# Moving four weight loads, a gather and a small table around the hand-over from the front part to the experts

## What is computed

```python
x = x + mix @ p['w_out']                       # output product, K = 1024
x = x + _moe(_rmsnorm(x, p['norm2_g']), p)

# _moe, for the tokens t (520 x 1024)
gl = t @ p['w_router_group'] + p['b_router_group']      # 4 groups, the best one
el = t @ p['w_router_expert'] + p['b_router_expert']    # 8 experts in it, the best two
...
for e in range(N_EXPERTS):                              # 32
    a = t @ p['w_gate'][e]                              # 1024 x 512
    u = t @ p['w_up'][e]                                # 1024 x 512
    out = out + combine[:, e:e + 1] * ((jax.nn.silu(a) * u) @ p['w_down'][e])
```

## Time and profile before

| | us |
|---|---|
| median of 3 executions | 777.6 (777.34 to 778.83) |
| the profiled execution's own time | 776.52 |
| its span, first to last instruction | 774.8 |
| PE busy | 668.8 (86%) |
| DVE busy | 272.4 (35%) |
| ACT busy | 160.7 (21%) |
| share of the span on the chain that ended last: PE, DMA, DVE | 46%, 34%, 9% |
| the weights' DMA queue (q1): moved, share of 16 engines | 233.95 MB, 75.3% |

### The profile page before, as it was taken

One profiled execution on the slowest core, in us unless ns is written; L12 is line 12 of the kernel. 1 busy time (PEld: TensorE's weight loads), 2 busy tenths in 40 slices (PEclk: granted clock), 3 DMA queues, 4 the chain that ended last, 5 costly groups with the idle time before them and its releaser, 6 DMA issues.

```text
span 774.8 us, 9756 instructions
## 1 busy us (share of the span) xinstructions
PE 668.8 (86%) x3294; PEld 333.8 (43%) x3294; DVE 272.4 (35%) x558; ACT 160.7 (21%) x314; POOL 89.4 (12%) x161
## 2 busy tenths in 40 slices
PE   6999989999996899999799987776778768888895
PEld 3488878954556533333233332222223322233231
DVE  7798994284476312121112121111111111112047
ACT  3677410421513001111001010010010101001023
POOL 4100000000000111212021211111121111021000
PEclk9999999999997799999999999999989999899998
DMA  9422016379217899999999999999999999999982
GB/s 332 183 109 110 1 53 278 117 290 383 91 61 287 309 353 377 412 389 415 382 419 397 408 412 408 415 406 411 413 393 415 401 412 408 402 403 415 422 331 110
DMA packets 29575, 246.56 MB, mean 318 GB/s; under 512 B 6578, under 2 KB 7090, under 8 KB 16592
## 3 DMA queue, kind: packets, MB, share of 16 engines
q1 hardware_dynamic: 22784, 233.95, 75.3%
q0 software_dynamic: 5280, 8.20, 3.1%
q10 hardware_dynamic: 1456, 3.62, 1.2%
HBM read 235.65 MB, written 19.20 MB: 329 GB/s over the span
## 4 chain that ended last, share of the span: by engine, by line
PE 46%; DMA 34%; DVE 9%; issue 3%; ACT 3%; PEldq 2%; ACTq 0%; PEld 0%; SPq 0%; POOLq 0%; DVEq 0%; POOL 0%
DMA mem<-in_w_down 33%; PE psA L1351 25%; PE psB L1351 20%; DVE mem L688 5%; PEldq L1684 2%; DMA mem<-hn_d,mem 1%; DVE mem L827 1%; PE psA L1356 1%; DVE mem L839 1%; ACT mem L629 1%; DVE mem L869 0%; DVE mem L870 0%; ACT front_c L618 0%; PEldq L1682 0%; ACT mem L566 0%
## 5 line engine op out<-in xcount | busy, mean ns | idle before, releaser
L1351 PE MATMUL psA<-mem 128*64 128x512 f32 (+8 forms) x1380 | 323.6, 528 | 43.6 <-DMA mem<-in_w_gu 12.4
L1351 PE MATMUL psB<-mem 128*64 128x512 f32 (+6 forms) x1242 | 274.4, 536 | 41.0 <-DMA mem<-in_w_gu 20.9
L1351 PEld LDWEIGHTS psA<-mem 128*64 128x64 f32 (+4 forms) x1380 | 154.2, 156 | 194.2 <-issue 163.8
L1351 PEld LDWEIGHTS psB<-mem 128*64 128x64 f32 (+2 forms) x1242 | 118.2, 153 | 178.9 <-issue 146.6
L688 DVE TENSOR_TENSOR mem<-mem 128x512 f32<-128x512 f32 (+18 forms) x121 | 66.0, 560 | 24.4 <-ACT mem L535 20.1
L1258 POOL DMA_INDIRECT y_d<-front_c,mem x30 | 27.5, 917 | 298.2 <-DVE front_c L1063 298.2
L1088 DVE TENSOR_TENSOR front_c<-front_c,psB 64x512 f32<-64x512 f32 x15 | 10.3, 690 | 136.1 <-ACT front_c L618 136.1
L1088 DVE TENSOR_TENSOR front_c<-front_c,psA 64x512 f32<-64x512 f32 x15 | 10.3, 690 | 124.6 <-ACT front_c L618 124.6
L1253 POOL DMA_INDIRECT mem<-hn_d,mem x34 | 33.4, 981 | 99.8 <-DMA hn_d<-mem 71.4
L618 ACT ACTIVATE front_c<-psA 64x512 f32<-64x512 f32 x15 | 8.8, 589 | 131.6 <-PE psA L1351 131.6
L618 ACT ACTIVATE front_c<-psB 64x512 f32<-64x512 f32 x15 | 8.8, 589 | 131.0 <-PE psB L1351 131.0
(11 more groups left out here) (232 smaller groups left out, 382.0 us busy)
## 6 DMA issues: line engine op xcount, KB each, us to landing
mem<-in_w_gu SPq DMA_DIRECT2D x64, 2048.0 KB, 36.6
mem<-in_w_down SPq DMA_DIRECT2D x32, 2048.0 KB, 41.8
mem<-in_w_out SPq DMA_DIRECT2D x2, 2048.0 KB, 8.4
y_d<-mem SPq DMA_DIRECT2D x1, 4096.0 KB, 11.8
mem<-y_d SPq DMA_DIRECT2D x8, 512.0 KB, 9.5
mem<-in_x_T SPq DMA_DIRECT2D x8, 260.0 KB, 8.7
mem<-in_w_vb SPq DMA_DIRECT2D x8, 256.0 KB, 8.9
mem<-in_x_prompt SPq DMA_DIRECT2D x4, 512.0 KB, 11.1
```

The lines of the kernel that those rows point to most:

```text
L1351: return nc.tensor.matmul(out, lhsT, rhs, start=start, stop=stop, skip_group_check=True)
```

## The change

Five things are moved.

1. SP issues `load(6)` after a new signal, `wo_used`: PE gives it when the last product that reads slot 6 is done, `out_half(3, 1, (1,))`. It no longer waits for the whole output product.
2. SP issues `load(7)` after the last store of `x2` and after the last logits (`lg_ps`), `load(8)` directly behind it once `hn2` is stored, and `load(9)` only when the rows of expert 0 have landed (`xg_in[0]`).
3. On PE the second table goes behind the turn of expert 0's rows. 12 matmuls of `keep_busy` stand ahead of the three register loads and 8 behind them; before, 8 stood ahead of the table and 14 behind the loads. The loads wait for the count alone (`xslot_rdy` 1), the table for both signals (`xslot_rdy` 2).
4. On DVE the copy of expert 0's turned rows goes ahead of `rows_of(tblx)`.
5. The signal `zero_rdy` is merged into `consts`; what waits for it waits for the same instruction as before.

The diff, without the list of semaphores that loses `zero_rdy`:

```diff
--- before.py
+++ after.py
@@ -242,6 +242,7 @@
         y_ps, y_ev, ya_rdy, sqa_rdy, suma_ps, rta_rdy, mixa_rdy = map(
             sem, "y_ps y_ev ya_rdy sqa_rdy suma_ps rta_rdy mixa_rdy".split())
         o_ps, o_ev, o_sc = sem("o_ps"), sem("o_ev"), sem("o_sc")
+        wo_used = sem("wo_used")
         n2sq, n2rt, hn2_rdy, rest_in, x2T_ps, x2T_ev, lg_ps, lg_ev, wr_rdy, rt_rdy = map(
             sem, "n2sq n2rt hn2_rdy rest_in x2T_ps x2T_ev lg_ps lg_ev wr_rdy rt_rdy".split())
         hn2_out = [sem(f"hn2_out{u}") for u in range(2)]
...
@@ -345,7 +346,7 @@
             for r in range(2):
                 sp.dma_start(o[2 + r], hfin[:, r]).then_inc(st_out, 16)
                 sp.dma_start(o[4 + r], hnew[:, r]).then_inc(st_out, 16)
-            sp.wait_ge(zero_rdy, 1)
+            sp.wait_ge(consts, 5)
             sp.dma_start(y2_d[0:1024, :].rearrange("(a p) n -> p a n", p=128), zeros.unsqueeze(1).to_broadcast([128, 8, D])).then_inc(zero_out, 16)
             sp.dma_start(y2_d[1024:2 * NTOK, :], zeros[0:2 * NTOK - 1024]).then_inc(zero_out, 16)
             sp.wait_ge(ub_ps, 4)
@@ -377,16 +378,17 @@
                 load(q)
             for n in range(NT - 1):
                 store_x2(n)
+            sp.wait_ge(wo_used, 1)
+            load(6)
+            store_x2(NT - 1)
             sp.wait_ge(o_ps, NT)
-            load(6)
+            sp.wait_ge(lg_ps, NT)
             load(7)
-            store_x2(NT - 1)
-
-            sp.wait_ge(lg_ps, NT)
             sp.wait_ge(hn2_out[0], 48)
             sp.wait_ge(hn2_out[1], 32)
             load(8)
             sp.wait_ge(x2_out, 16 * NT)
+            sp.wait_ge(xg_in[0], 16)
             load(9)
 
             for q in range(NSLOT, 3 * NE):
@@ -1037,7 +1039,7 @@
             link(V.tensor_scalar(xt, xt, MAGIC, None, ALU.add))
             link(V.tensor_scalar(xt, xt, -MAGIC, 0.0, ALU.add, ALU.max))
             link(V.tensor_tensor_scan(xs, one32, xt, 0.0, ALU.mult, ALU.add))
-            V.tensor_copy(xb[0:1, 1:NE + 1], xs[0:1])
+            V.tensor_copy(xb[0:1, 1:NE + 1], xs[0:1]).then_inc(xslot_rdy, 1)
             link(tt(d, xs, xt, ALU.subtract))
             link(tt(xprod, oh12.rearrange("p t j e -> p (t j) e"), d.unsqueeze(1).to_broadcast([128, 2 * NT, NE]), ALU.mult))
             first, tile = xtile[:, 0, :], xtile[:, 1, :]
@@ -1093,9 +1095,9 @@
                 x1 = dve.value_load(xb[0:1, bass.ds(s + 1, 1)], min_val=0, max_val=NX)
                 further(x0, x1, ps, other)
 
+            xT_copy(0, 0)
             dve.wait_ge(xtbl_ps, 1)
             rows_of(tblx, psA[:, 3, 128:512], NX + 1).then_inc(xtbl_rdy, 1)
-            xT_copy(0, 0)
             dve.wait_ge(xtbl_rdy, 1)
             dve.wait_ge(ex_out, 1)
             link(V.tensor_reduce(R(1), ex[:, :, 0:NG], AX.X, ALU.add))
@@ -1231,7 +1233,7 @@
             G.memset(H[:, :, :, NS:NS + 1], 0.0).then_inc(h0_rdy, 1)
 
             pool.wait_ge(s_ev, NH)
-            G.memset(zeros, 0.0).then_inc(zero_rdy, 1)
+            G.memset(zeros, 0.0).then_inc(consts, 1)
             pool.wait_ge(st_out, 16 * 5)
             pool.wait_ge(rta_rdy, 1)
             G.iota(tokens, [[1, NTOK]], base=0, channel_multiplier=0, allow_small_or_imprecise_dtypes=True).then_inc(tokens_rdy, 1)
@@ -1552,7 +1554,7 @@
             pe.wait_ge(lg_ev, 1)
             out_half(3, 1, (0,))
             turn(3, 2)
-            out_half(3, 1, (1,))
+            out_half(3, 1, (1,)).then_inc(wo_used, 1)
             logits(3, 2)
             out_half(3, 0, (0,))
             pe.wait_ge(slot_rdy, 2)
@@ -1581,7 +1583,7 @@
             pe.wait_ge(tbl_rdy, 1)
 
             def further_table():
-                pe.wait_ge(xslot_rdy, 1)
+                pe.wait_ge(xslot_rdy, 2)
                 for n, (t, j) in enumerate(itertools.product(range(NT), range(2))):
                     r = ROWS[t]
                     ins = mm(psA[0:C, 3, 128:128 + 2 * (NX + 1)], row_oh[0:r, t, j, :], xentry[0:r, 2 * t + j].rearrange("p x w -> p (x w)"),
@@ -1684,12 +1686,13 @@
                     pe.drain().then_inc(gu_used, 1)
                 further(x0, x1, ps, other, s, s + 2, half_used if split else None)
 
+            keep_busy(12)
+            pe.wait_ge(xslot_rdy, 1)
+            bounds = [pe.value_load(xb[0:1, k:k + 1], min_val=0, max_val=NX) for k in range(3)]
             keep_busy(8)
-            further_table()
-            bounds = [pe.value_load(xb[0:1, k:k + 1], min_val=0, max_val=NX) for k in range(3)]
-            keep_busy(14)
             pe.wait_ge(xg_in[0], 16)
             x_T(psA[:, 0, :], xg[0:C, 0, :]).then_inc(xgT_ps, 1)
+            further_table()
             tile_step(0, before=False, split=True)
             pe.wait_ge(cw3_rdy, 1)
             for n, (t, j) in enumerate(itertools.product(range(NT), range(2))):
```

More of the change, by code:

```diff
@@ L259, in build @@
         y_in = [sem(f"y_in{t}") for t in range(NT)]
-        x2_out, zero_rdy, zero_out, tokens_rdy, cw3_rdy, cw_ps, picks_rdy, rest_out, y_last = map(
-            sem, "x2_out zero_rdy zero_out tokens_rdy cw3_rdy cw_ps picks_rdy rest_out y_last".split())
+        x2_out, zero_out, tokens_rdy, cw3_rdy, cw_ps, picks_rdy, rest_out, y_last = map(
+            sem, "x2_out zero_out tokens_rdy cw3_rdy cw_ps picks_rdy rest_out y_last".split())
         f_acc, f_ps, f_sum, f_sq, f_rt, f_done, f_out = map(sem, "f_acc f_ps f_sum f_sq f_rt f_done f_out".split())
```

## The result

| | before | changed |
|---|---|---|
| median, 20 executions each (us) | 776.99 (775.01 to 781.43) | 771.11 (767.02 to 777.46) |
| ratio to before, 95% interval | | 0.9926 (0.9912 to 0.9941) |
| profiled execution / its span | 776.52 / 774.8 | 770.57 / 768.9 |

The change makes the kernel 5.9 us faster. The direction was right and the size was less than half of what came.

What follows compares the result with a forecast made beforehand. Bound by the weight stream, whose early loads follow expert 0's first transpose on PE: -2.6 there and +0.2 for the clock give -2.4 us, from a median of 777.6 to 775.2; range 772.8 to 777.7.

Steps and rivals of the forecast that it cites:

- What bounds the kernel: Weight stream, saturated from 290 to 730; ahead of it, whatever moves the first transpose moves the end by as much.
- PE up to the first transpose: From the fillers' start at 248.47 to expert 0's first transpose: at 257.8 and not 260.42, so -2.6 us.
- The register loads: Three on PE between the two groups of fillers: 1.43 us, as in the old chain, ending at 254.5.
- The 20 fillers: On PE ahead of the first transpose: first 8 take 2.95, four more 1.6, last 8 3.3 at the low clock.
- rival 1: PE's clock is up for the last fillers, transpose 3.7 to 4.9 us earlier: 773.3 us; chance 0.22.
- The gather: Expert 0's rows: starts at 249.4, lands between 252.8 and 258.3, taken as 254, hidden behind the fillers.
- Unit 6's place: Load issued at 223.37, 9.5 us ahead of 232.88, in a stretch of idle DMA: gain and cost 0.
- the hold on unit 9: Unit 9 held back until the gather lands; by the queue rule it buys the gather nothing.
- The clock behind the transposes: Transposes at the low clock cost 0 to 0.7 us more, taken as 0.2.
- rival 2: Clock comes back late, behind 257.8; gain shrinks to 1.6 or nothing: 776.9 us; chance 0.15.
- Rival 4: Earlier PE start is not passed on, stream short of something else up to 286: 777.6 us; chance 0.12.
- rival 3: Slower: low clock through expert 0's gate/up product, 14.8 and not 7.4, sum +5.5: 783 us; chance 0.06.

Runs made afterwards that it cites:

- e6: Changed kernel with 2 fillers ahead of the three register loads and 18 behind, not 12 and 8: 776.9 us, ratio 0.9997.
- e2: Changed kernel with the loads of units 6 to 9 where they stood before, only PE's and DVE's new order kept: 778.0 us, ratio 1.0022.
- e3: Changed kernel without unit 9's wait for the gather: 777.6 us, ratio 1.0014.
- e12: Changed kernel with 2 and not 8 fillers behind the register loads: 771.8 us, ratio 0.9923.
- e8: Changed kernel with units 8 and 9 both held for the gather, and 2 and not 8 fillers behind the register loads: 772.5 us, ratio 0.9931.
- e11: Changed kernel with unit 6 loaded only at the end of the output product, as before: 777.2 us, ratio 0.9997.
- e1: Kernel before with only SP's part of the change (the new places of the loads): 777.2 us, ratio 1.0001.
- e9: Changed kernel measured once more with no edit, for a second profile: 772.1 us, ratio 0.9924.
- e5: Changed kernel with 28 and not 8 fillers behind the register loads: 776.1 us, ratio 0.9981.
- e4: Changed kernel with unit 7 loaded at the end of the output product, ahead of the last x2 store: 774.3 us, ratio 0.9975.

## Why the prediction was wrong in size

**What bounds the kernel: right.** The stream after 290 is untouched (1.01 and 406 GB/s in both), and the time follows the holes ahead of it. In the changed kernel unit 10, unit 13 and the span moved by 6.1, 6.4 and 5.9.

**The step that failed is "PE up to the first transpose".** Its sum was 2.95 + 1.6 + 1.43 + 3.3 = 9.3 from the start of the fillers. Measured:
- The register loads were priced at 1.43 and cost 0.40 and 0. The 1.43 of the earlier trace rows was the uncovered part of 2.31 from the table's signal on, after the table's own matmuls. I called them the same code; the code is, what stands in the queue ahead of it is not. Behind 12 fillers only 0.40 of the 2.2 is uncovered, or nothing; e6 brings the idle time back (2.13).
- The 20 fillers were priced at 7.85, with the low clock from 249 on as in the earlier trace rows. They took 4.99 in the first profile, where no low spell touched them, and 6.75 in the second. Whether a low spell comes at all is chance: with nearly the same pauses ahead of the fillers, the changed kernel's first profile, e2, e3 and e12 had none there. How long it lasts goes with the pauses in it. Before, the fillers began at 248.47, the clock fell at 249.4, PE paused for 1.10 and 1.43, and the clock was back at 259.7. In e8 the fillers began at 248.47 too and the clock fell at 249.4 too, but the 14 fillers were one piece, and it was back at 252.8. The forecast took the clock from the old execution and at once removed a pause that had prolonged its low spell.

With T = 6.4 to 6.7 for 9.4 the sum of the prediction becomes -5.3 to -5.6 before any loss from the clock, against the measured -5.9. The forecast's own place for this was rival 1, at 3.7 to 4.9 with a chance of 0.22. It had the clock right and kept the 1.43, and its 0.28 for a filler at the full clock was high: 12 took 2.94, or 0.245 each. The 6.4 and 6.7 are of two profiles with different clocks, so the miss is no luck; but the 12.0 of before is of one profile alone. With a shorter low spell it could have been as little as 10.9 (an estimate: its gather landed at 259.3).

**The gather: right, and closer to the path than I had it.** It was put at 254 and within 252.8 to 258.3. It landed at 252.58, 5.5 after its start and 6.4 behind the row numbers, where the forecast had 5.6 (254 - 248.4), and was the last to come, 0.96 behind the fillers.

**Unit 6's place was costed at 0 and the hold on unit 9 had no price of its own, and both are wrong as statements on their worth.** In themselves they bring nothing that PE reads early. But unit 6's place makes the store of `hn2` take 3.4 and not 12.5 (e11), and the hold makes the gather take 5.5 and not 9.9 (e3); without either the whole gain goes. The prediction had the first in its own working (2.7 for 11.8) and did not say that its result hangs on it. For the hold, the Trainium skill's rule on queues ("DMA: Bandwidth & Descriptors", Queues, rings and completion order) was read to mean that holding back unit 9 buys the gather nothing, while the 254 counted on it. e3 shows 4.3 us at the transpose. Taking turns does not make the gather independent of what is queued beside it: with a unit issued just ahead (before, e2, e11) or three in flight (e3) it took 7.7 to 9.9 us, with two and the last of them issued 6.6 to 8.8 us ahead 5.5 or less (the changed kernel, e1, e9).

**The clock behind the transposes** was put at 0 to 0.7 of loss. It was 1.7 in the first profile, in the gate/up product (3.4 us at the low clock). That is the size of rival 2 but not its mechanism: the clock did not come back late, it was full through fillers and transposes and fell afresh at 255.1. In the second profile the loss was 0 there, and expert 1's product lost 1.7. The table inside the pause for the copy cost nothing: from the first transpose to the product it was 1.49, before 1.48. The first fall of the clock came at 235.8, 238.0 and 236.2 in the three profiles of the two kernels. The Trainium skill ("TensorE: Matmul & The Clock Gate", What's actually happening) says of the point at which the clock comes up that it differs between executions of one kernel. The trace agrees, and here the fall differs too: 238.0 and 236.2 are of the same kernel.

**Rival 4** (the start is not passed on) is refuted by e5, **rival 3** (slower) did not come, though e2 shows its mechanism: a late gather, a fallen clock and 0.2% slower.

## What to carry to other kernels

Where several things must be early for one start, each half alone can measure as zero. Taking away unit 6's place or the hold gave back the whole, and moving the table back gave back two fifths. Try such changes together, and then one out at a time. A small transfer on the path (a store, a gather) wants the large loads issued well ahead of it or held until it has landed, though not more of them than the stream can make up. Before you price a register load from a row, measure from its signal and look at what the queue still holds then; before you price a filler, look at the clock of that row and at the pauses beside it.

## What the runs showed of the hardware that was not expected

- A 0.5 MB store to HBM took 3.0 to 3.5 us with no load in flight when it started (3.4 in the changed kernel, where one of 2 MB left 1.1 behind it), 8.1 with one issued 4.8 ahead (e4), 11.8 with two ahead, and 12.5 with one ahead and one 1.0 behind (e11).
- Three register loads on PE left it idle for 1.43 behind ten short matmuls that had waited, 2.13 behind 2 fillers, 0.40 or nothing behind 12, and 0.49 behind 12 and the table. In all of these where PE was idle, the next matmul started 2.2 to 2.3 us behind the signal.
- The clock fell although PE never paused for more than 1.43 us: in the kernel before at 249.4, behind pauses of 1.12, 0.45 and 1.43 with short work between them (the earlier trace rows show the last and the fall):

```profile
243.99 0.44 PE L1351 MATMUL psA<-ohb,oneb 128*128 128x32 bf16 x4 [1.12 <-DVE ohb L688]
...
246.43 0.61 PE L1351 MATMUL psA<-mem 128*64 128x64 bf16 x10 [0.45 <-DVE mem L688]
```

  In the changed kernel, e2, e3 and e12 nearly the same pauses (1.00 to 1.08, 0.45, 1.43) brought no fall there.
